# First input tile projected from unnormed x, with the first loads reordered and two weight splits moved to VectorE

## The reference, cut to what matters

```
h = rmsnorm(x, norm1_w)          # x * rsqrt(mean(x*x) + eps) * w, per token
proj = h @ w_in                  # z, xBC, dt, u (512 wide), q, k, v, three gates of 1024
y_b, s5_new = s5_mixer(proj[..., OFF_U:OFF_Q], ...)       # state-space mixer, fed by u
gates = sigmoid(proj[..., OFF_GATE:])
```

## Time and profile before

| what | value |
|---|---|
| timed runs | 1684.84, 1685.16 and 1686.6 us, median 1685.16 |
| profiled execution, first to last instruction | 1684.5 us |
| PE busy | 1654.0 us (98%) |
| DVE, ACT, POOL busy | 966.9, 556.0 and 791.2 us |
| DMA | 146 GB/s on average |

### The profile page before, as it was taken

One profiled execution on the slowest core, in us unless ns is written; L12 is line 12 of the kernel. 1 busy time (PEld: TensorE's weight loads), 2 busy tenths in 40 slices (PEclk: granted clock), 3 DMA queues, 4 the chain that ended last, 5 costly groups with the idle time before them and its releaser, 6 DMA issues. The chain is left out here.

```text
span 1684.5 us, 30884 instructions
## 1 busy us (share of the span) xinstructions
PE 1654.0 (98%) x12241; PEld 1604.7 (95%) x12241; DVE 966.9 (57%) x1642; ACT 556.0 (33%) x1240; POOL 791.2 (47%) x756
## 2 busy tenths in 40 slices
PE   7999999999999999999999999999999999999997
PEld 7999999999999998888899999999999999999997
DVE  6859811406634554778873289666665565744346
ACT  5332121342213332543411154443443333322233
POOL 5483122322221111141322325877777777787774
PEclk9999999999999999999999999999999999999998
DMA  5364363232233234434365431543433344966443
GB/s 209 84 127 133 104 203 98 89 92 91 87 93 103 89 130 134 161 115 140 126 218 191 152 126 42 180 162 145 151 141 141 141 167 165 367 224 267 162 187 103
DMA packets 95805, 245.85 MB, mean 146 GB/s; under 512 B 14369, under 2 KB 42273, under 8 KB 95417
## 3 DMA queue, kind: packets, MB, share of 16 engines
q1 hardware_dynamic: 73824, 174.48, 30.5%
q0 software_dynamic: 10256, 33.59, 6.7%
q10 hardware_dynamic: 11592, 35.96, 6.3%
HBM read 177.11 MB, written 66.65 MB: 145 GB/s over the span
## 5 line engine op out<-in xcount | busy, mean ns | idle before, releaser
L1642 PE MATMUL ps<-HL,WH 128*128 128x384 f32 (+1 forms) x1536 | 507.7, 331 | 4.4 <-DVE HL L691 1.8
L1643 PE MATMUL ps<-HH,WL 128*128 128x384 f32 (+1 forms) x1536 | 497.4, 324 | 0.0
L1644 PE MATMUL ps<-HH,WH 128*128 128x384 f32 (+1 forms) x1536 | 496.3, 323 | 0.0
L1642 PEld LDWEIGHTS ps<-HL,WH 128*128 128x128 f32 x1536 | 289.4, 188 | 15.6 <-issue 9.3
L1643 PEld LDWEIGHTS ps<-HH,WL 128*128 128x128 f32 x1536 | 289.7, 189 | 0.3
L1644 PEld LDWEIGHTS ps<-HH,WH 128*128 128x128 f32 x1536 | 289.6, 189 | 0.0
L1285 POOL TENSOR_TENSOR WL<-WRAW,WH 128x1024 fp32r<-128x1024 f32 x59 | 145.0, 2457 | 243.3 <-DMA WH<-in_w 243.3
L1282 POOL DMA_DIRECT2D WH<-in_w x59 | 34.6, 586 | 354.4 <-PE ps L1644 352.9
L2932 DVE TENSOR_TENSOR X<-X,ps 128x528 f32<-128x528 f32 (+2 forms) x170 | 107.9, 656 | 155.5 <-PE ps L2238 104.6
L2327 ACT ACTIVATE GT<-ps 128x384 f32<-128x384 f32 (+1 forms) x72 | 33.4, 465 | 215.5 <-PE ps L1644 183.5
L2932 DVE TENSOR_TENSOR RB<-RB,ps 128x528 f32<-128x528 f32 x60 | 42.1, 701 | 103.4 <-ACT RB L2847 85.9
(11 more groups left out here) (467 smaller groups left out, 4266.2 us busy)
## 6 DMA issues: line engine op xcount, KB each, us to landing
WRAW<-in_w SPq DMA_DIRECT2D x75, 512.0 KB, 3.4
ffn_scratch<-STG SPq DMA_DIRECT2D x70, 528.0 KB, 3.6
WH<-in_w POOLq DMA_DIRECT2D x62, 512.0 KB, 4.6
SOP<-ffn_scratch SPq DMA_DIRECT2D x36, 528.0 KB, 7.9
gate_scratch<-GT ACTq DMA_DIRECT2D x24, 528.0 KB, 3.2
PX<-gate_scratch ACTq DMA_DIRECT2D x22, 528.0 KB, 4.2
HL<-ffn_scratch SPq DMA_DIRECT2D x22, 528.0 KB, 10.4
RAWB<-in_w SPq DMA_DIRECT2D x10, 1024.0 KB, 6.2
```

The source lines that it names most:

```text
L1642: nc.tensor.matmul(out, wh, rl, start=start, stop=False)
L1643: nc.tensor.matmul(out, wl, rh, start=False, stop=False)
L1644: return nc.tensor.matmul(out, wh, rh, start=False, stop=stop)
```

## The change

- SP loads in another order: slice 0 of x, then columns 0 to 255 of units 0 and 1 together (piece 0), slice 1, columns 256 to 511 (piece 1), slices 2 and 3, columns 512 to 1023 (piece 2), the other slices, units 2 and 3, x's second chunk; then the small tables and the third chunk.
- u of the first 384 tokens is made from x times norm weight, without the root. ACT writes `HH` of it, DVE `HL`, in one instruction each. DVE multiplies by the spread root when it moves u out of PSUM (`evict_first_u_dve`). The split of the normed first chunk, which the gates need, comes last, after the third chunk's.
- The second chunk's squares are made first: six by ACT, two by DVE, added in wide instructions (`x_second_sum_dve`). ACT makes the first chunk's eight squares after them. The sums and spreads of all three chunks now stand inside the u pairs.
- DVE makes the low parts of units 0 to 5; POOL only counts them.
- On PE, gate 0 takes chunks 1 and 2 before 0, and the gates, taps and transposes are interleaved otherwise.

```diff
+    def x_plain_high_act(k):
+
+        nc.scalar.wait_ge(s_x[k], 16)
+        if k == 0:
+            nc.scalar.wait_ge(s_par, 16)
+        nc.scalar.mul(HH[:, k, 0:384], X0[:, k, 0:384], prm("norm1", k, 1)).then_inc(xp_hi, 1)
+
+    def x_plain_low_dve(k):
+
+        dve = nc.vector
+        dve.wait_ge(xp_hi, k + 1)
+        dve.scalar_tensor_tensor(HL[:, k, 0:384], X0[:, k, 0:384], prm("norm1", k, 1), HH[:, k, 0:384].bitcast(F32),
+                                 ALU.mult, ALU.subtract).then_inc(xp_lo, 1)
+
...
+    def x_first_squares_act(ks):
+
+        for k in ks:
+            nc.scalar.activation(SQ0[:, k, :], X0[:, k, 0:384], ACT.Square).then_inc(pq_done, 1)
+
+    def x_first_add_dve(i):
+
+        dve = nc.vector
+        if i == 0:
+            dve.wait_ge(pq_done, SECOND_BY_ACT + KD)
         else:
-            nc.vector.tensor_tensor(x_square_at(0, k), X0[:, k, 0:384], X0[:, k, 0:384], ALU.mult).then_inc(pq_used, 1)
+            dve.wait_ge(x0_add, i)
+        if i < 2:
+            n = 4 >> i
+            dve.tensor_tensor(SQ0[:, 0:n], SQ0[:, 0:n], SQ0[:, n:2 * n], ALU.add).then_inc(x0_add, 1)
+        else:
+            dve.tensor_tensor(ACC[:, 0:384], SQ0[:, 0], SQ0[:, 1], ALU.add).then_inc(x0_add, 1)
...
+    def x_second_sum_dve():
+
+        dve, pairs = nc.vector, GT[:, 0:768].rearrange("p (k c) -> p k c", c=384)
+        dve.wait_ge(pq_done, 4)
+        dve.tensor_tensor(SQ[:, 0:2], SQ[:, 0:2], SQ[:, 2:4], ALU.add).then_inc(pq_used, 1)
+        dve.wait_ge(s_xc[1], 128)
+        dve.tensor_tensor(pairs, X0[:, 6:8, 384:768], X0[:, 6:8, 384:768], ALU.mult).then_inc(pq_used, 1)
+        dve.wait_ge(pq_used, 2)
+        dve.tensor_tensor(SQ[:, 0:2], SQ[:, 0:2], pairs, ALU.add).then_inc(pq_used, 1)
+        dve.wait_ge(pq_done, SECOND_BY_ACT)
+        dve.wait_ge(pq_used, 3)
+        dve.tensor_tensor(SQ[:, 0:2], SQ[:, 0:2], HF0[:], ALU.add).then_inc(pq_used, 1)
+        dve.wait_ge(pq_used, 4)
+        dve.tensor_tensor(ACC[:, 384:768], SQ[:, 0], SQ[:, 1], ALU.add).then_inc(pq_used, 1)
...
+
+        dve = nc.vector
+        dve.wait_ge(r0_ok, 1)
+        dve.wait_ge(acc_done[0], j + 1)
+        dve.tensor_tensor(as_steps(UF[:, j, :], 0, 3), as_blocks(u_bank(j, 0), 3), as_blocks(GT[:, 0:384], 3),
+                          ALU.mult).then_inc(acc_free[0], 1)
...
+                dve.wait_ge(r0_ok, 1)
+                dve.wait_ge(acc_done[0], 4)
+            else:
+                dve.wait_ge(pn_rs, ROOT_ORDER.index(n) + 1)
             if i >= 2:
...
+        def first_piece(q):
+            c = PIECES[q]
+            sp.dma_start(WRAW[:, :, c], io["w"][0:2, :, c].rearrange("u p n -> p u n")).then_inc(s_piece[q], 16)
+
+        x_chunk(0, [0])
+        first_piece(0)
+        x_chunk(0, [1])
+        first_piece(1)
+        x_chunk(0, [2, 3])
+        first_piece(2)
+        x_chunk(0, [4, 5, 6, 7])
+        first_weights(2)
+        first_weights(3)
+        x_chunk(1)
         sp.dma_start(HOT[:], io["hot"]).then_inc(s_hot, 16)
         sp.dma_start(RTAB[:], io["rtab"]).then_inc(s_hot, 16)
-        first_weights(0)
-        first_weights(1)
-        first_weights(2)
-        x_chunk(1, range(4))
-        x_chunk(1, range(4, KD))
-        first_weights(3)
         x_chunk(2)
         sp.dma_start(PRM[:, NPAR_FIRST:NPAR], io["params"][:, NPAR_FIRST:NPAR]).then_inc(s_par_rest, 16)
...
+        def first_lows_counted():
+
+            pool.wait_ge(half_ok, 5)
+            pool.sem_inc(split_ok, 4)
+
+        def gate_lows_counted():
+
+            pool.wait_ge(half_ok, 7)
...
+        s5_rows()
+        s5_squarings(0)
+        gate_lows_counted()
+        s5_squarings(1)
+        u = 6
         while u < FFN + 2:
...
-                pe.wait_ge(acc_free[0], 1)
-                pe.wait_ge(h_lo, 2 * KD)
             for k in range(KD):
                 if j == 0:
-                    pe.wait_ge(h_lo, KD * n + k + 1)
-                if j == 0 and n == 0 and k in (0, 4):
...
         u_pair(0, 0)
-        pe.wait_ge(bias_ev, 2)
-        u_pair(2, 0, {1: lambda: x_sums_pe(1), 3: lambda: x_spread_pe(1)})
-        u_pair(0, 1)
-        u_pair(2, 1, {1: lambda: x_sums_pe(2), 3: lambda: x_spread_pe(2)})
+        u_pair(2, 0, {4: lambda: x_sums_pe(1), 6: lambda: x_spread_pe(1)})
+        u_pair(0, 1, {0: lambda: x_sums_pe(0), 3: lambda: x_spread_pe(0)})
+        u_pair(2, 1, {3: lambda: x_sums_pe(2), 4: lambda: bias_by_distance(0), 5: lambda: x_spread_pe(2),
+                      6: lambda: bias_by_distance(1)})
...
-        gate(0, [2])
         taps(1)
-        gate(1, [0])
+        gate(1, [2])
         taps(2)
-        gate(1, [1])
         taps(3)
-        gate(1, [2])
+        gate(2, [0])
         stt_rows(0)
-        for n in range(3):
-            gate(2, [n])
-            stt_rows(n + 1)
+        stt_rows(1)
+        gate(2, [1])
+        stt_rows(2)
+        gate(2, [2])
+        stt_rows(3)
         gate(3, [0])
         step_sums(0, 0)
...
-        for k in range(0, KD, 2):
-            x_first_square(act, k)
+        x_plain_high_act(0)
+        high_piece(0)
+        x_plain_high_act(1)
+        act.wait_ge(ar_ok, 1)
+        nc.scalar.activation(SF("mag"), SF("ar"), ACT.Exp).then_inc(mag_ok, 1)
+        high_piece(1)
         nc.scalar.activation(SF("unused_root")[:, 0:1], ZERO[:], ACT.Sqrt)
-        high_half(0)
-        x_root_act(0)
-        high_half(1)
-        x_split_act(0, 2)
-        x_squares_act(1, range(2))
-        x_split_act(2, 3)
+        x_plain_high_act(2)
+        x_plain_high_act(3)
+        high_piece(2)
+        for k in range(4, KD):
+            x_plain_high_act(k)
         high_weights(2)
-        x_split_act(3, 4)
-        x_squares_act(1, range(2, 4))
-        x_split_act(4, 5)
         high_weights(3)
-        x_split_act(5, 6)
-        bias_rows(0)
-        x_split_act(6, 7)
-        bias_rows(1)
-        x_split_act(7, 8)
-        x_squares_act(1, range(4, KD))
+        x_squares_act(1, range(SECOND_BY_ACT))
+        x_first_squares_act(range(KD))
         x_root_act(1)
         act.wait_ge(red_ok, 1)
         nc.scalar.activation(SF("sin"), SF("r"), ACT.Sin)
         nc.scalar.activation(SF("cos"), SF("r2"), ACT.Sin).then_inc(sin_ok, 1)
-        x_squares_act(2, range(4))
-        x_split_act(8, 11)
-        evict_u(0, 0)
...
-        x_split_act(11, 13)
-        evict_u(1, 0)
-        x_split_act(13, 16)
-        x_squares_act(2, range(4, KD))
-        evict_u(2, 0)
-        evict_u(3, 0)
-        x_root_act(2)
+        nc.scalar.activation(SF("unused_root")[:, 0:1], ZERO[:], ACT.Sqrt)
+        for k in range(KD):
+            x_split_act(k, k + 1)
+            if k == 1:
+                x_root_act(0)
+            if k == 5:
+                x_root_copy_act()
+            x_squares_act(2, [k])
         evict_u(0, 1)
         evict_u(1, 1)
-        x_split_act(16, 24)
+        x_root_act(2)
+        x_split_act(8, 10)
+        bias_rows(0)
+        bias_rows(1)
+        x_split_act(10, 12)
         evict_u(2, 1)
+        x_split_act(12, 14)
         evict_u(3, 1)
+        x_split_act(14, 18)
+        high_weights(4)
+        evict_u(0, 2)
+        x_split_act(18, 19)
+        evict_u(1, 2)
+        x_split_act(19, 21)
+        high_weights(5)
+        x_split_act(21, 23)
+        evict_u(2, 2)
+        evict_u(3, 2)
+        x_split_act(23, 24)
         for j in range(4):
-            evict_u(j, 2)
-            if j == 1:
-                high_weights(4)
-                high_weights(5)
+            act.wait_ge(acc_free[0], j + 1)
             act.wait_ge(acc_free[2], j + 1)
             act.dma_start(uscr[j * P:(j + 1) * P, :], UF[:, j, :]).then_inc(s_ust, 16)
...
+        def low_piece(q):
+
+            c = PIECES[q]
+            dve.wait_ge(first_high, q + 1)
...
+
+        x_plain_low_dve(0)
+        low_piece(0)
+        x_plain_low_dve(1)
+        low_piece(1)
+        x_plain_low_dve(2)
+        x_plain_low_dve(3)
+        low_piece(2)
+        for k in range(4, KD):
+            x_plain_low_dve(k)
+        for u in (2, 3):
+            dve.wait_ge(first_high, u + 2)
+            tt(high_low(u)[1], WXR[:, u - 2, :], high_low(u)[0].bitcast(F32), ALU.subtract).then_inc(half_ok, 1)
         dve.wait_ge(den_ok, 1)
         nc.vector.reciprocal(SF("den"), SF("den")).then_inc(den_inv, 1)
-        x_split_dve(8, 16)
-        x_add_dve(2, range(KD))
+        x_second_sum_dve()
+        x_first_add_dve(0)
+        x_recip_dve(1)
+        x_first_add_dve(1)
+        x_first_add_dve(2)
+        x_split_dve(0, 3)
+        x_recip_dve(0)
+        x_split_dve(3, 8)
+        x_third_sum_dve()
+        for j in range(2):
+            evict_first_u_dve(j)
         x_recip_dve(2)
-        x_split_dve(16, 24)
+        for j in range(2, 4):
+            evict_first_u_dve(j)
+        x_split_dve(8, 18)
+        dve.wait_ge(first_high, 6)
+        tt(high_low(4)[1], WRAW[:, 0, :], high_low(4)[0].bitcast(F32), ALU.subtract).then_inc(half_ok, 1)
+        x_split_dve(18, 21)
```

(37 more changed lines are left out.)

197 lines of the change are left out of this document (79 added, 118 removed).

## The result

The changed kernel takes 1695.24 us (median of 4 runs, 1693.37 to 1696.72) against 1685.26 for the kernel before beside it: 10.0 us slower, a ratio of 1.0058 with a 95% interval of 1.0043 to 1.0072. The forecast was 1684.8 in a range of 1681.4 to 1688.8. The profiled execution has a span of 1694.2 us, 9.7 more than the earlier trace rows.

The account below looks back on a forecast made before the run. PE, busy 98% of the span, was taken to bound the kernel, so only its gaps could be won. The early gain is given back by gate 2's second chunk (105.7 against 105.83); 0.3 us gain gives 1684.8 us, range 1681.4 to 1688.8.

Parts of the forecast that it names:

- First product: PE's first large product starts at 6.8 (6.3 to 7.6) in place of 17.30; the 10.5 us are not kept.
- pairs: First two u pairs on PE: the slow clock start is hidden, and PE is through its products at 22.5.
- second chunk's sum: DVE has the second chunk's squares added at 25.4; PE waits 2.9 us and starts that chunk at 30.75.
- gate 0: PE starts gate 0 at 65.9 in place of 69.16, 3.2 us earlier; 67.5 with one clock fall.
- The clock behind that sum: One fall of PE's clock behind the 2.9 us wait costs 1.6 us: second chunk at 32.4, gate 0 at 67.5.
- DVE ahead of the taps: DVE's extra splits free it at 71.3 (72.9 with the fall), before 59.84; W is ready at 86.7.
- the taps: PE arrives 20.0 us after gate 0's start, at 87.5; taps start at 87.5 to 88.9, at best 86.0.
- POOL in the taps' term: POOL excluding DVE during W's products: only small squarings and unit 6's subtraction come there, adding 0 to 2.2 us.
- the sum: Closing total: gate 2's second chunk at 105.7 against 105.83, 0.3 us of gain taken, nothing to add behind.
- u's way back: Stores of u land at 79.6, unit 7 at 102.6; ACT's queue behind it puts gate 2's second chunk at 105.7.
- the one on the slower side: u comes back late: stores near 81.5, unit 7 at 105.9, gate 2's second chunk 109.0 to 110; 1689 us, chance 0.16.
- Nothing behind the point: After gate 2's second chunk starts (105.83 before), the code is the same and PE-bound, so no further time is added.

Follow-up runs that it names:

- experiment 3: Kernel before, with POOL's first two parts of the small squarings ahead of unit 6's subtraction instead of behind it: 1695.95 us, ratio 1.007.
- experiment 8: Changed kernel with the wait for the second chunk's sum filled by 12 unread products and the taps apart, squarings still ahead of unit 6: 1696.1 us.
- experiment 9: Changed kernel with POOL's small squarings behind unit 7's subtraction, the wait for the second chunk's sum filled and the taps apart: 1687.0 us, ratio 1.0005.
- experiment 10: Changed kernel with only POOL's order altered, small squarings behind the subtractions of units 6 and 7: 1688.9 us, ratio 1.0023.
- experiment 5: Changed kernel with the small squarings ahead of POOL's memsets and the wait for the second chunk's sum filled by 12 unread products: 1697.3 us, ratio 1.0068.
- experiment 7: Changed kernel with the small squarings ahead of POOL's memsets, the wait for the second chunk's sum filled and the taps apart: 1698.4 us, ratio 1.0073.
- experiment 11: Changed kernel with POOL's small squarings behind unit 7's subtraction and the wait for the second chunk's sum filled, taps in pairs: 1686.7 us, ratio 1.0004.

## Why the prediction was wrong

- **First product, pairs, second chunk's sum, gate 0:** right. 6.77 against 6.8; sums at 24.5 against 25.4; second chunk's first product at 30.09 against 30.75; gate 0 at 66.18 against 65.9, the figure without a fall of the clock.
- **The clock behind that sum:** counted as one fall of 1.6 us. The profile of the changed kernel has none, but five of six profiles with this wait unfilled (1.2 to 2.6 us long) have one, and none of five with it filled. Gate 0 is at 69.2 to 69.6 where 2.0 to 2.6 us were waited and at 68.0 and 68.3 where 1.4 and 1.2 were, against 66.2 to 66.7 without a fall: 2 to 3 us. So such a wait does bring a fall in most profiles, and it costs more than was counted. In the profiled execution the counted fall did not come, which is luck for the figures that follow. Nor is the fall of the earlier trace rows certain: behind the same 1.95 us of 8-column products it came in five of the 13 profiles.
- **DVE ahead of the taps, and the taps:** right. W's first product at 71.11 (71.3), its last ending at 84.8 (86.7 at most), so PE came to the taps without a wait, at 87.15 against 87.5. That match is partly luck: gate 0 was 1.3 us earlier than counted (67.5, with the fall), and PE took 21.0 us from there in place of 20.0.
- **The step that failed is POOL in the taps' term:** "POOL now comes to that place only with small squarings and with unit 6's subtraction, so 0 to 2.2 are added", and in the sum "POOL's squarings are earlier, but PE did not wait for them". I priced the exclusion of the earlier trace rows in one direction only, POOL holding up DVE. It works the other way at least as hard: between DVE's long products a small instruction gets in about once for each. Twelve squarings, 3 us when DVE is idle, take 18.5 (82.77 to 101.25). That they stood ahead of a subtraction that PE needs at 97.6 was in POOL's queue for anyone to read; I counted their busy time, not their place. It cost 6.33 us of waiting and 2.63 of slow clock; experiment 3 reproduces it in the kernel before (a wait of 8.27), experiments 8 and 9 differ in this alone and lose 10.0 and 1.3 us, and experiment 10 brings the change's loss from 10.0 to 3.1 us with POOL's order alone.
- **u's way back:** "this term was slack for PE and now ends last". Unit 7 was rounded at 101.11, 1.5 us earlier than I had it: the first load of u went out at 76.86 and not at 79.6, and unit 7 was there 24.2 us behind it, where 23.0 were counted. Two errors offset each other in part. In experiment 9, with POOL out of the way, PE waits 0.42 for ACT's copies and the point is 104.16 against 105.7. ACT's queue does end last there, as said, but unit 7's rounding is through at 101.65, and the tanh behind it was released at 102.23 by a gate's store. Unit 7 becomes the dear one when POOL's memsets slip (experiments 5 and 7).
- **Rivals:** the one on the slower side gave 1689, 6 us short, and had another mechanism. (Its stores issued at 72.3 with 5.7 and 2.7 us give 80.7, not the 81.5 it uses.) None had POOL's order in it.
- **Nothing behind the point:** 2.5 us came there, 1.3 of them around a fall of the clock at 1058 that the kernel before did not have in its profile.

The Trainium skill ("SBUF — State Buffer", section "SBUF: two separate sides") says that the shared port pair is an exclusive lock, held for a whole instruction, and that the loser fully blocks. The rows agree: a squaring lasts until DVE's product beside it is over. In the 17.5 us of these products about one squaring got in for each of them.

What stays open: where the slower six of experiment 9's eleven runs lose their 3 us. Only one of its executions was profiled. The kernel before has such runs too, five of 27 beside it above 1687 us. The 0.9 us of loss that experiment 11 keeps are within the interval.
